# Hybrid retention and DeltaNet layers: a weight load moved from SyncE's queue to ScalarE's in the first unit of a layer, and one block of exponentials placed three slots later

## What is computed

```
for l in range(2):
    h = rmsnorm(x, norm_g)
    proj = h @ w_in                                  # 1024 x 9232
    rq, rk, rv, rz, dq, dk, dv, dz, db, da, gr, gd = split(proj)
    o_r = group_norm(retention(rope(rq), rope(rk), rv)) * silu(rz)     # 4 heads
    dq, dk, dv = silu(causal_conv(dq, dk, dv))                         # 4 taps
    o_d = gated_deltanet(l2norm(dq), l2norm(dk), dv, beta(db), g(da))  # 8 heads, chunks
    o_d = rms(o_d) * dn_g * silu(dz)
    y = sigmoid(gr) * (o_r @ w_up_r) + sigmoid(gd) * (o_d @ w_up_d)
    x = x + y @ w_o
return rmsnorm(x, final_gain)
```

## Time and profile before

| | |
|---|---|
| time of 3 runs, median (lowest to highest) | 2777.66 us (2776.64 to 2779.44) |
| time of the profiled execution | 2776.54 us |
| its span in the trace | 2774.7 us |
| PE busy | 2695.4 us, 97% |
| DVE busy | 1737.1 us, 63% |
| POOL busy | 884.3 us, 32% |
| ACT busy | 561.4 us, 20% |
| granted TensorE clock, mean | 0.996 |
| weight loads through line 536 | 142 from `in_w_in`, 3.8 us to landing (median) |

### The profile page before, as it was taken

The page is one execution under the profiler, slowest core; times in us unless marked ns, Lnnn a source line. Parts: engine busy times, 40 slices in busy tenths (PEclk is TensorE's granted clock), DMA queues, the critical chain, the costliest instruction groups (busy, mean ns, idle before and its releaser), DMA issues.

```text
span 2774.7 us, 38181 instructions
## 1 busy us (share of the span) xinstructions
PE 2695.4 (97%) x14098; PEld 2249.2 (81%) x14098; DVE 1737.1 (63%) x3818; ACT 561.4 (20%) x1207; POOL 884.3 (32%) x469
## 2 busy tenths in 40 slices
PE   7899999999999999999998999999999999999998
PEld 5788888888888888788877888888888888887886
DVE  5788878877854333433577797888887434443333
ACT  5222222222211111200132222222222111121001
POOL 3323232333321121435442232333333121143443
PEclk9999999999999999999999999999999999999999
DMA  4322222222221112333532322222222111133244
GB/s 165 92 63 65 71 81 62 62 73 81 64 54 35 41 37 66 122 95 111 163 90 71 80 60 72 70 77 70 62 74 72 46 41 38 40 99 104 92 134 143
DMA packets 288476, 217.71 MB, mean 78 GB/s; under 512 B 31426, under 2 KB 245780, under 8 KB 288036
## 3 DMA queue, kind: packets, MB, share of 16 engines
q1 hardware_dynamic: 255330, 154.39, 20.5%
q10 hardware_dynamic: 32962, 60.89, 6.4%
HBM read 176.37 MB, written 38.86 MB: 78 GB/s over the span
## 4 chain that ended last, share of the span: by engine, by line
PE 57%; DVE 21%; DMA 10%; issue 6%; SPq 3%; POOL 3%; ACT 1%; DVEq 0%; POOLq 0%; ACTq 0%
PE dense_ps L714 15%; PE dense_ps L718 15%; PE dense_ps L716 15%; DMA arena<-l_scratch 6%; SPq L595 3%; DVE arena L1593 2%; DVE arena L1833 2%; DVE arena L1836 2%; PE work L697 2%; DMA l_scratch<-arena 1%; DVE arena L1607 1%; POOL arena L2148 1%; PE work L925 1%; PE work L905 1%; DMA w_raw<-in_w_in 1%
## 5 line engine op out<-in xcount | busy, mean ns | idle before, releaser
L714 PE MATMUL dense_ps<-act_hi,w_hi 128*128 128x512 f32 x2816 | 1170.5, 416 | 14.6 <-POOL act_lo L2077 5.1
L718 PE MATMUL dense_ps<-act_hi,w_lo 128*128 128x512 f32 x2816 | 1103.2, 392 | 0.0
L716 PE MATMUL dense_ps<-act_lo,w_hi 128*128 128x512 f32 x2816 | 1101.3, 391 | 0.0
L2064 POOL TENSOR_TENSOR w_lo<-w_raw,w_hi 128x1024 fp32r<-128x1024 f32 x192 | 495.4, 2580 | 1331.2 <-DVE w_hi L1470 1331.2
L718 PEld LDWEIGHTS dense_ps<-act_hi,w_lo 128*128 128x128 f32 x2816 | 529.4, 188 | 117.1
L714 PEld LDWEIGHTS dense_ps<-act_hi,w_hi 128*128 128x128 f32 x2816 | 532.1, 189 | 109.4 <-issue 11.0
L716 PEld LDWEIGHTS dense_ps<-act_lo,w_hi 128*128 128x128 f32 x2816 | 532.7, 189 | 88.9 <-issue 0.2
L1593 DVE SCALAR_TENSOR_TENSOR arena<-arena,cols 128x512 f32<-128x512 f32 x288 | 273.9, 951 | 5.0
L1470 DVE CAST w_hi<-w_raw 128x1024 fp32r<-128x1024 f32 x192 | 135.0, 703 | 220.0 <-PE dense_ps L718 190.7
L697 PE MATMUL work<-mk,arena 128*128 128x128 f32 x896 | 130.8, 277 | 11.9 <-issue 7.5
L1833 DVE TENSOR_TENSOR arena<-arena 128x60 f32<-128x60 f32 (+14 forms) x480 | 103.5, 216 | 49.7 <-DMA arena<-l_scratch 37.4
(11 more groups left out here) (199 smaller groups left out, 3211.9 us busy)
## 6 DMA issues: line engine op xcount, KB each, us to landing
w_raw<-in_w_in SPq DMA_DIRECT2D x142, 512.0 KB, 3.8
arena<-l_scratch SPq DMA_DIRECT2D x32, 512.0 KB
gate_scratch<-arena ACTq DMA_DIRECT2D x64, 256.0 KB, 2.6
arena<-gate_scratch ACTq DMA_DIRECT2D x64, 256.0 KB, 3.2
w_raw<-in_w_out SPq DMA_DIRECT2D x18, 512.0 KB, 4.1
arena<-row_scratch SPq DMA_DIRECT2D x32, 256.0 KB, 5.3
o_scratch<-arena ACTq DMA_DIRECT2D x32, 256.0 KB, 2.0
arena<-o_scratch ACTq DMA_DIRECT2D x32, 256.0 KB, 3.5
```

The lines of the kernel that those rows point to most:

```text
L714: eng.matmul(dense_ps[:, to, :], w_hi[:, slot, k, :], hi[:, k, seg], start=(k == 0), stop=False)
L716: eng.matmul(dense_ps[:, to, :], w_hi[:, slot, k, :], lo[:, k, seg], start=False, stop=False)
L718: mm = eng.matmul(dense_ps[:, to, :], w_lo[:, slot, k, :], hi[:, k, seg], start=False, stop=(k == KT - 1))
L2064: eng.tensor_tensor(w_lo[:, slot, :, :], w_from[second][:, :, :], w_hi[:, slot, :, :].bitcast(F32), ALU.subtract)\
```

## The change

The load of K of head 1 leaves SyncE's queue. It is issued from ScalarE's, in the step that takes the second half of R out of PSUM, ahead of that step's own waits. It has the same wait, for POOL's split of R. And `dec 1` moves from slot 19 to slot 22. Both happen once in each layer.

```
@@ unit_schedule, first unit
         at(18, "mask", 1)
-        at(19, "dec", 1)
+        at(22, "dec", 1)
         solve, spread_at, vt = 20, 25, 35
@@ SyncE
                 l_load(0)
                 row_load(0, 1)
-                load_w(n + BLK_HEADS, w_src(l, w_in, DK0 + P))
                 l_blocks(1, 1)
                 load_w(n + BLK_HEADS + 1, w_src(l, w_in, DZ0))
@@ ScalarE, evac of D and R
                                 a = "DR".index(of)
+                                if kind == "first" and a and half:
+                                    eng.wait_ge(w_lo_ok.sem, w_lo_ok.after(n + BLK_HEADS, 0))
+                                    eng.dma_start(w_raw[:, :, :], w_src(l, w_in, DK0 + P)).then_inc(w_in_ok.sem, 16)
                                 eng.wait_ge(dense_ok[half].sem, dense_ok[half].after(gg, 1))
```

## The result

The changed kernel takes 2789.01 us (median of 8 runs, 2784.45 to 2794.32), the kernel before 2781.18 us (8 runs on the same chips, 2776.64 to 2784.41). The ratio is 1.0033, with a 95% interval of 1.0021 to 1.0044. So the change costs 0.33%, some 9 us. A later run on another chip gave 1.0044 (1.0031 to 1.0056), some 12 us. The forecast was 2788.7 us, +0.40% or 11.0 us. That the two times differ by only 0.3 us is partly luck: the kernel before took 2781.18 us beside the changed one, 3.5 us more than in the three runs on which the forecast was built. It is the differences that have to be compared, 11.0 us with 9 and 12. The profiled execution took 2784.45 us, which is 7.9 us more than that of before (2776.54).

What follows compares the result with a forecast made beforehand. TensorE, busy 97%, was taken as the bound, with DVE's slackless chain from K's cast to Z's setting the waits. 5.1 + 4.9 + 0.7 + 0.3 = 11.0 us on 2776.54, plus 1.1 for the median, gave 2788.7 us; range 2783.5 to 2795.

Steps and rivals of the forecast that it cites:

- The load of K is asked for too late: On ScalarE's queue K is issued after DVE wants it; its cast comes +5.1 us late in layer 0, +4.9 in layer 1.
- 0.7 (at most 1.4) for the clock: Layer 1, product needing `spread`: a stall grown to 3.21 us may lower TensorE's clock, 0 to 1.4 us, taken as 0.7.
- SyncE's freed entry is worth nothing: Taking the load of K out of SyncE's queue frees no one, as `l_store` behind it waits for `nl 1`: 0 us.
- the cover moves with the delay: DVE's 6.11 us idle before Z's cast can't hide 5.1 us, since Z's load is issued 7.36 us after K's cast.
- rival (b): Z's load keeps its time, so DVE's 6.11 and 7.55 us of idleness absorb the delay: 2777.7 us, chance 0.06.
- The landing of Z: Time from issue to landing of Z's load, 10.0 us beside `l_load`, a store and the 1 MB rope table.
- The chain above moves as a whole: Cast of K, `nl 1`, 8 stores, `l_load`, load and cast of Z: 17.36 us in layer 0, 18.80 in layer 1, without slack.
- its own sign of being wrong: DVE's wait before Z shrinking by what the new wait takes, or the load of K under way before 98 us.
- rival (d): Z landing faster as the rope table comes later, or a tidier clock, gives back 2 to 3 us per layer; chance 0.09.
- `dec 1` gains nothing: Start of R: waits of 0.27 and 1.36 us go, but those before `spread` grow to 2.15 and 3.21: gain 0.
- The clock: Longer TensorE stalls can cost clock: 0.7 us before `spread` and 0.3 us behind Z's wait; could be 0 or 2.2 us.
- The 0.3 us for a longer stall behind the wait for Z: Layer 0: TensorE's 2.63 us stall for the first state grows, slowing the products after it; 0.3 us taken of 0.75.

Runs made afterwards that it cites:

- experiment 2: Only the load of K moved to ScalarE's queue, `dec 1` left in slot 19, against the kernel before: 1.0039 (1.0027 to 1.0051).
- experiment 4: `dec 1` in slot 22, load of K on SyncE's queue but held until ScalarE's tanh is done, against the kernel before: 1.0039 (1.0024 to 1.0055).
- experiment 10: Load of K on ScalarE's queue, early, in the evacuation of D's second half, `dec 1` in slot 19, against the kernel before: 0.9996 (0.9984 to 1.0007).
- experiment 7: The kernel before with only the rope table asked for one unit later on ScalarE's queue, against the kernel before: 1.0000 (0.9990 to 1.0011).
- experiment 8: The full change with the rope table asked for one unit later, against the kernel before: 1.0057 (1.0039 to 1.0075).
- experiment 9: The full change run again, against the kernel before: 1.0044 (1.0031 to 1.0056).
- experiment 6: The full change plus the load of Z ahead of `l_load`, against the kernel before: 1.0016 (1.0004 to 1.0028), 2776.75 us.
- experiment 5: The kernel before with only the load of Z put ahead of `l_load`, against the kernel before: 0.9966 (0.9954 to 0.9977), 2760.77 us against 2771.16.
- experiment 11: Load of Z ahead of `l_load`, `dec 1` in slot 22, load of K on SyncE's queue, against the kernel before: 0.9958 (0.9942 to 0.9974).

## Why the prediction was right

- **The load of K is asked for too late.** It was forecast for 102.1 with 4.0 us to landing, so the cast at 106.1. It came at 101.98 with 4.1 us, and the cast at 106.08: +5.06 us where the forecast had +5.1. In layer 1 the cast is 12.95 us later than in the trace of before, of which 6.2 stood before the layer began, so 6.7 us. The forecast had 4.9, and 0.7 (at most 1.4) for the clock. It kept the last tanh at its old place in the layer; it came 2.1 us later (1478.05 for 1469.72, less 6.2), through the longer wait before `spread` and the low clock behind it. Experiments 2, 4 and 10 confirm the step from three sides: the load alone makes the loss, on either queue, and in time on ScalarE's it makes none.
- **SyncE's freed entry is worth nothing,** and the cover moves with the delay. `l_store`, `l_load` and Z's load are all 5.1 us later, and 7.37 us lie between K's cast and Z's load, as before. This is what rival (b), the hidden delay, had against it.
- **The landing of Z was mis-sized.** "The chain above moves as a whole" took Z's 10.0 and 11.4 us over unchanged. They became 8.2 and 8.0 us, since TensorE's new wait and the low clock behind it hold back the evacuation of R, and with it the rope table. Experiments 7 and 8 bear this out: with the table gone from beside it Z takes 8.3 to 8.9 us in both kernels, and the difference between them is gone. So 3.3 and 2.7 us came through in the profile instead of 5.1 and 4.9 plus clock. DVE's wait for Z was forecast to stay at 6 to 7 us and was 3.28. By its own sign of being wrong, a wait before Z that shrinks by what the new wait takes, the forecast is half wrong in layer 0 (2.8 of 5.75 us) and mostly wrong in layer 1 (4.3 of 5.25 us). That is rival (d), which had a chance of 0.09. It doesn't come every time (layer 1 of experiment 9: 11.7 us to landing, 4.8 us lost), and the time, +0.33% and +0.44%, lies on both sides of the forecast +0.40%. The mechanism was right, and that the size came out so close is in part luck, since this term was too high, and the delay of layer 1's last tanh, 2.1 us where 0.7 were allowed, too low.
- **`dec 1` gains nothing:** TensorE's wait moved to `spread`, as forecast. The waits became 2.57 and 4.04 us for 2.15 and 3.21; the evacuation of D no longer holds TensorE up at all.
- **The clock.** In layer 1 the fall came behind the 4.04 us (product at line 887 in 1.99 us) and in the profile of experiment 9, with 2.92 us, it didn't. The 0.3 us for a longer stall behind the wait for Z had the wrong sign: no wait of TensorE shows there any more, and in layer 1 the stretch from line 955 to 966 (954 to 965 after) took 8.91 us (1498.58 to 1507.49) instead of 9.74. What the forecast had no term for is the fall behind TensorE's new wait, 6 us at half clock. In the full change the wait for Z hides it. In experiment 6, without this wait, it shows as 2.2 and 1.7 us.

## What to carry to other kernels

When a load moves to another engine's queue, read when that engine gets there in its own order, and compare this with when its reader starts: here 101.98 against 101.02. An idle stretch covers a delay only if what ends it doesn't hang on the delayed instruction. Where the long idle stretch itself stands in the trace, ask what ends it: swapping two neighbours on SyncE's queue gained 0.34%. And before a transfer is moved out of the way of a load, look which load it will stand beside then: the rope table one unit later gained 1.1 and 2.6 us in the landing of Z, and nothing in the time.

## What the runs showed of the hardware

- A load of 512 KB behind an `l_load` of the same size on the same queue landed in 8.0 to 11.7 us, and in 4.0 to 4.7 ahead of it (experiments 5, 6 and 11). `l_load` behind it made nobody wait in five of the six stretches, and DVE for 4.30 us in the sixth (experiment 11, layer 1).
- A table of 1 MB going out 0.62 us behind an `l_load` on the other queue: DVE waited 3.13 us for that `l_load`, and 1.11 us without the table (experiment 7 and the kernel before).
- A DMA issue on ScalarE goes out beside a running tanh, 0.02 us after its start.
- Stalls of TensorE of 4.08 and 4.01 us before line 928 were followed by about 6 us at 1.2 GHz in the full change, in both layers of the first profile. Between the layers the clock stayed at 2.4 GHz (granted clock 1.00 in every 10 us from 130 to 1440). Stalls of 1.65 to 2.9 us before `spread`'s product were followed by either level, the seven of 3.15 to 4.04 us by the low one each time.
